# Decode part of a hybrid mLSTM and sparse-attention step: loads and stores in another order, and two compressions inside the state loop

## The chip, the cores and the metric

The kernel runs on one core of a Trainium2 chip. The core has five engines that run their own instruction streams and meet at semaphores: TensorE (PE in the rows; PEld is its weight load), VectorE (DVE), ScalarE (ACT), GpSimd (POOL) and SyncE (SP). SP does no arithmetic; it issues the transfers between HBM and the on-chip memory. ACT can issue transfers too, on a queue of its own. A row whose engine is SPq or ACTq is such an issue. The metric is the time of one execution on the device in microseconds; lower is better.

## The reference, cut to what matters

One layer, for two groups of requests that share the weights: a prompt of 1024 tokens, and a decode group of 8 requests ("samples") with 4 new tokens each, 32 rows in all, over a cache of 1024 tokens per sample. The part that the change touches is the decode group:

```python
# mLSTM heads: a matrix state per sample b and head h, 128 x 128
num = einsum('bthd,..', w, vc) + inter * einsum('bhvk,bthk->bthv', C, qc)   # needs C transposed
C   = decay * C + einsum('bsh,bshv,bshk->bhvk', wk, vc, kc)                 # the state update

# sparse attention heads: three branches over the cache
past_cmp = cache_kv_cmp[layer, page_table]                    # 8 pages of 128 tokens per sample
first, second = cmp_sub(past_cmp, w_cmp)                      # compression: einsum('bnpchd,cpde->bnche')
kv_c = compress_blocks(...)                                   # then scores on kv_c, top-16 blocks,
o = g0 * o_compressed + g1 * o_selected(cache_kv_sel) + g2 * o_window(cache_kv_win)

y = concat(h_m * silu(z_m), o_n * silu(z_n)) @ w_out          # merge, for prompt and decode rows
out = x + rmsnorm(y, g_post)
```

`w_out` is 1024 x 1024 in float32, 4 MB. The merge of the prompt's 1024 rows needs it whole.

## The kernel before, in words

The program is written by hand, one instruction stream for each engine (`@block.sync`, `@block.gpsimd`, `@block.scalar`, `@block.vector`, `@block.tensor`); nothing reorders it. Every stream runs in the order of its text, and a `wait_ge` holds up all that stands behind it on that engine. The prompt is projected and its attention done first. The decode part begins near 860 us of the profiled span, and runs in four stages.

1. **Set-up, 864 to 905 us.** SP loads the decode rows, the four heads of the matrix state (`c_in[h]`, 512 KB each, to `c_all[h]`), and the pages of `cache_kv_cmp` of sample b (`load_cmp(b)`, L700 to L706: 8 transfers of 128 KB, each with the page number read from the page table into a register first, L697). They go to one of four slots, `cms`: three in the big buffer WR, the fourth in a piece of XT called `pairs3`. POOL sorts a loaded sample (`sort_sample`), and counts it in `cm_sorted`. (The count has one more than the samples sorted, since the prompt's own block is counted too.)
2. **Compression.** For pair q (sample q-1) PE turns the sorted block (`turn_sample`, L2051, 16 transposes; in two halves of 8 by the program's own order), ACT copies it out of PSUM (`take_sample`, L1115), PE multiplies by the compression weights (`sample_products`, L2068, two groups of 8 matmuls, counted in `cmp_done`), DVE adds the shifted halves (`sum_sample`, L1529 and L1531), PE turns the values (`turn_values`, L2078) and DVE copies them (`take_values`, L1539). q = 1 to 5 stand in the set-up; q = 6 to 8 and the last products stand behind the state loop.
3. **State loop, 905 to 931 us.** For each of 4 heads: PE transposes the state of the 8 samples into banks 2 and 3 (L2275), ACT copies that to `ct_h` (L1236), DVE spreads the keys (`kblk`, L1707) and multiplies the old state by its decay (`c_dec`, L1714), PE forms the update in four matmuls that use 32 rows each and write banks 0, 1, 4 and 5 (L2284), DVE adds it (L1720, counted in `cn_ready`), and PE makes the numerator (L2287, L2290: 8 matmuls 4 columns wide, counted in `num_done`). SP stores the new state (L781).
4. **Attention over the selected and window pages, and the merge, 959 us to the end.** Two groups of four samples. PE's stream is a list of attention steps ("gates", "cmp", "u0" to "u11", ...), and `fill(n)` puts n matmuls of the merge (L2326, 512 columns wide) between them; 128 such in all. `fill` waits for `wo_in` at its first matmul (chunks 0 to 5 of `w_out` in WR) and for `wo_late` at its seventh (chunks 6 and 7, whose place holds the compression weights until the last compression). Step "u0" waits until 32 pages of `cache_kv_sel` have landed (`page_in`; four buffers, one over the state of heads 0 and 1, one over heads 2 and 3, two free earlier). DVE's first piece of the merge (`scale_rows`, L1748 and L1750) waits for the last small loads of SP (`gp_in`).

What sets the order of the transfers is SP's text. Behind the state loop it reads: chunks 0 to 3 of `w_out` (L730), stores of the state (L781), the last page loads (L713), which wait until all four heads are stored, then chunks 4 and 5 and chunks 6 and 7 (L734), windows (L725), `g_post` (L800), rows of `x` (L803) and eight small loads (L806, L807).

## Time and profile before

| | us |
|---|---|
| median of 3 runs | 1140.92 |
| lowest and highest | 1140.73, 1146.22 |
| the profiled execution, its own time | 1149.3 |
| its span, first to last instruction | 1147.5 |
| PE busy in it | 1063.9 (93%) |
| DVE, ACT, POOL busy | 474.1, 337.0, 68.5 |
| mean granted clock of TensorE | 0.957 |

The profile gives busy time by engine, groups of instructions by line, and, on asking, every instruction in order of time with the idle time before it and what ended that. "Granted clock" is the share of TensorE's full 2.4 GHz that the chip let through; 0.50 is 1.2 GHz. All terms below are sums within the profiled execution, whose own time is 8.4 us above the median of the runs.

### The profile page before, as it was taken

How to read it: one execution, taken by the hardware profiler on the slowest of the kernel's cores; microseconds unless marked ns; L12 is line 12 of the kernel's file. 1: busy time of each engine (PE TensorE's matmuls, PEld its weight loads, DVE VectorE, ACT ScalarE, POOL GpSimd, SP SyncE). 2: the span in 40 equal slices, each digit the busy share in tenths (PEclk: the TensorE clock that was granted, in tenths of full speed). 3: DMA queues.
4: the chain of work that ended last, by engine and by line, in shares of the span. 5: the costliest groups of instructions: out<-in, count | busy, mean ns of one | idle time of the engine just before them, and what ended most of it. 6: DMA issues, size and time to landing. Idle time of an engine off the chain costs nothing.

```text
span 1147.5 us, 14594 instructions
## 1 busy us (share of the span) xinstructions
PE 1063.9 (93%) x5369; PEld 640.9 (56%) x5369; DVE 474.1 (41%) x1045; ACT 337.0 (29%) x816; POOL 68.5 (6%) x173
## 2 busy tenths in 40 slices
PE   5999999999999999999978999999998893599997
PEld 4556654444445555786654456666567793245443
DVE  6444440000121221223247777677664532244442
ACT  5321110000011111111036676767665220022121
POOL 1000000000000000120011000001005100000000
PEclk9999999999999999999979999999998767799999
DMA  9302020203020151521031000000005344722512
GB/s 331 139 2 74 1 73 1 66 28 76 1 76 19 29 117 33 121 58 51 1 97 51 2 1 2 1 1 2 1 1 155 105 142 147 220 87 93 189 37 79
DMA packets 84205, 77.62 MB, mean 68 GB/s; under 512 B 29394, under 2 KB 68734, under 8 KB 84070
## 3 DMA queue, kind: packets, MB, share of 16 engines
q1 hardware_dynamic: 73654, 65.12, 18.9%
q10 hardware_dynamic: 10480, 11.57, 3.9%
q8 instruction: 43, 0.70, 0.2%
q14 instruction: 28, 0.23, 0.1%
HBM read 66.72 MB, written 14.10 MB: 70 GB/s over the span
## 4 chain that ended last, share of the span: by engine, by line
PE 77%; SPq 9%; DVE 6%; issue 3%; ACT 2%; DMA 2%; ACTq 0%; POOL 0%; DVEq 0%; POOLq 0%
PE PS L2021 26%; PE PS L2014 13%; PE PS L2326 8%; PE PS L2135 6%; PE PS L2154 5%; PE PS L2167 5%; SPq L697 2%; SPq L706 2%; SPq L713 1%; DMA out_s_C<-KVN 1%; PE PS L2355 1%; PE PS L2141 1%; PE PS L2186 1%; DVE XT L1582 1%; DMA KTR<-in_x_sample 1%
## 5 line engine op out<-in xcount | busy, mean ns | idle before, releaser
L2021 PE MATMUL PS<-WR,XT 128*128 128x512 f32 (+1 forms) x768 | 306.9, 557 | 0.0
L2021 PEld LDWEIGHTS PS<-WR,XT 128*128 128x128 f32 x768 | 144.0, 190 | 147.7 <-issue 144.6
L2014 PE MATMUL PS<-XT,WR 128*128 128x352 f32 x576 | 173.9, 463 | 2.1 <-ACT QN L1028 2.1
L2014 PEld LDWEIGHTS PS<-XT,WR 128*128 128x128 f32 x576 | 109.7, 192 | 63.0 <-ACT QN L1028 2.6
L1571 DVE TENSOR_REDUCE XT<-PS 128x1 f32<-128x640 f32 (+7 forms) x128 | 84.4, 701 | 30.2 <-PE PS L2141 29.7
L2326 PE MATMUL PS<-WR,QT 128*128 128x512 f32 x128 | 63.9, 621 | 24.5 <-DMA WR<-in_w_out 24.5
L2135 PE MATMUL PS<-KTR,XT 64*128 64x512 f32 (+3 forms) x384 | 84.8, 502 | 0.4 <-ACT XT L1149 0.2
L1149 ACT ACTIVATE XT<-PS,XT 128x640 f32<-128x640 f32 (+7 forms) x96 | 66.7, 701 | 10.6 <-DVE XT L1571 10.6
L2154 PE MATMUL PS<-cst,XT 128*128 128x128 f32 x396 | 62.1, 281 | 4.4 <-DVE XT L1582 3.6
L2326 PE MATMUL PS<-WR,KT 128*128 128x512 f32 x128 | 61.0, 598 | 0.0
L2135 PEld LDWEIGHTS PS<-KTR,XT 64*128 64x128 f32 x384 | 40.1, 192 | 28.4 <-issue 17.9
L1582 DVE TENSOR_SCALAR XT<-XT,small 128x640 f32<-128x640 f32 (+7 forms) x96 | 53.5, 557 | 3.5
L1162 ACT ACTIVATE MT<-PS 128x512 f32<-128x512 f32 (+3 forms) x96 | 41.1, 466 | 45.3 <-PE PS L2154 45.1
L2154 PEld LDWEIGHTS PS<-cst,XT 128*128 128x128 f32 x396 | 42.6, 142 | 17.8 <-issue 10.0
L1162 ACT ACTIVATE VV<-PS 128x512 f32<-128x512 f32 (+3 forms) x96 | 41.3, 469 | 32.0 <-PE PS L2154 31.9
L2326 PEld LDWEIGHTS PS<-WR,QT 128*128 128x128 f32 x128 | 23.2, 196 | 47.5 <-DMA WR<-in_w_out 24.6
L1407 DVE SCALAR_TENSOR_TENSOR KTR<-KTR,PS 128x512 f32<-128x512 f32 x8 | 5.5, 687 | 104.1 <-ACT KTR L1051 104.1
L2326 PEld LDWEIGHTS PS<-WR,KT 128*128 128x128 f32 x128 | 22.9, 192 | 23.5 <-issue 23.3
L2167 PE MATMUL PS<-MT,KVN 128*64 128x256 f32 x264 | 34.9, 390 | 0.8 <-ACT MT L1162 0.8
L1028 ACT ACTIVATE QN<-PS 128x352 f32<-128x352 f32 (+1 forms) x24 | 10.7, 457 | 84.1 <-PE PS L2014 83.2
L2167 PE MATMUL PS<-VV,KVN 128*64 128x256 f32 x264 | 35.1, 391 | 0.0
L1254 ACT ACTIVATE KTR<-PS 128x512 f32<-128x512 f32 x16 | 9.5, 594 | 85.7 <-PE PS L2326 85.6
(457 smaller groups left out, 1246.5 us busy)
## 6 DMA issues: line engine op xcount, KB each, us to landing
WR<-in_w_in SPq DMA_DIRECT2D x24, 512.0 KB, 7.9
WR<-in_cache_kv_cmp SPq DMA_DIRECT2D x48, 128.0 KB, 2.5
MT<-row_factors ACTq DMA_DIRECT2D x16, 256.0 KB, 7.3
WR<-in_w_in SPq DMA_DIRECT2D x32, 128.0 KB, 3.3
QN<-in_cache_kv_win SPq DMA_DIRECT2D x8, 512.0 KB, 7.6
out_y_prompt<-MT ACTq DMA_DIRECT2D x8, 512.0 KB, 2.9
out_s_kv_win<-in_cache_kv_win SPq DMA_DIRECT2D x1, 4064.0 KB
XT<-in_x_prompt ACTq DMA_DIRECT2D x6, 512.0 KB, 4.2
```

The lines of the kernel that those rows point to most:

```text
L697: return sp.value_load(table[0:1, b * NPG + n:b * NPG + n + 1], min_val=0, max_val=I["cache_kv_cmp"].shape[1] - 1)
L706: sp.dma_start(cms[b % 4][n % 2 * 64:n % 2 * 64 + 64, n // 2, :], src).then_inc(cm_s_in[b % 4], 16)
L1149: nc.scalar.activation(pp[p % 2][h][:, 0:nb * P], bank(score_bank(p, h), -(-nb // 4))[:, 0:nb * P], ACT.Exp, bias=nmax[:, u % 4:u % 4 + 1] ...
L1162: nc.scalar.activation(pt[q % 2][:, h, j:j + n, g % 2 * P:(g % 2 + 1) * P], bank(4 + y % 2)[:, 0:n * P].rearrange("p (k t) -> p k t", k=n) ...
L1571: nc.vector.tensor_reduce(nmax[:, u % 4:u % 4 + 1], bank(score_bank(p, h), -(-nb // 4))[:, 0:nb * P], AX.X, ALU.max, negate=True).then_inc ...
L1582: nc.vector.tensor_scalar(pp[p % 2][h][:, 0:nb * P], pp[p % 2][h][:, 0:nb * P], s1, gates[:, i, gc:gc + 1], op0=ALU.mult, op1=ALU.mult).th ...
L2014: ins = mm(b[:, 0:THIRD], w[:, k, r // 3 * P:(r // 3 + 1) * P], xt[:, k, r % 3 * THIRD:(r % 3 + 1) * THIRD], **f)
L2021: ins = mm(b[:, 0:width], xt[:, k, r * P:(r + 1) * P], w[:, k, :], **f)
L2135: mm(bank(score_bank(p, h) + j // 4)[:, 0:n * P], qz[r, i % 2, g, :], ktr[r, br, (k0 + j) * P:(k0 + j + n) * P], start=True, stop=not (j + ...
L2154: ins = nc.tensor.transpose(bank(4 + y % 2)[:, k * P:(k + 1) * P], pp[p % 2][h][:, (j + k) * P:(j + k + 1) * P], ident)
L2167: ins = mm(bank(6)[h * ND:(h + 1) * ND, x], v, pt[q % 2][:, h, k, :], start=False, stop=br == 1 and k == nb - 1, skip_group_check=True)
L2326: ins = mm(bank(2 + 3 * half), (qt if c < 4 else kt)[:, c % 4, i * P:(i + 1) * P], wo[:, c, half * 512:half * 512 + 512], start=c == 0, st ...
```

## The change

Five things, all in the decode part.

- **w_out by ACT.** Chunks 0 to 5 are issued by ACT, behind its work for the state loop, when all samples are sorted (`cm_sorted` 9). Chunks 6 and 7 stay with SP, and stand behind the windows.
- **SP's order.** Each head's state is stored among the page loads, pages over heads 0 and 1 wait only for the stores of these two, and so for 2 and 3; the page numbers of the first group are read into registers early (`held`, while SP has nothing else), and those of the second group at the place where SP waits for the first. Sample 7 is loaded to slot 0, not to slot 3, and before the page loads.
- **Buffers.** `pairs3` now holds two copies of the transposed state (`cts`), one for even and one for odd heads. `c_dec` and `kblk` move to STG.
- **The update** is two matmuls of 512 columns, in banks 2 and 3 that the transposes used, where it was four of 256 in four other banks. So PE's transposes of the next head wait for DVE's addition (`cn_ready`), and the update's matmuls wait for ACT's copies (`ct_ready`). The decode values are loaded to 2 groups of 32 partitions, where it was 4.
- **Compressions in the loop.** Banks 0, 1, 4 and 5 are free in the loop, and one half of `turn_sample` and one half of `sample_products` stand in each head: pairs 6 and 7 turned, pairs 5 and 6 multiplied.

```diff
+        cts = [pairs3[:, n * 1024:(n + 1) * 1024].rearrange("p (b k) -> p b k", b=SB) for n in range(2)]
+        slot = lambda b: b % 4 if b < 7 else 0
...
+            def store_state(h):
+                sp.wait_ge(cn_ready, h + 1)
+                sp.dma_start(O["s_C"][:, :, h, :, :].rearrange("l b v k -> v (l b) k"), c_all[h]).then_inc(c_in[h], 16)
...
-            held = [[page(4 + j, n) for n in range(NPG)] for j in range(4)]
+            held = [[page(j, n) for n in range(NPG)] for j in range(4)]
...
             load_cmp(7)
+            load_pages((3,))
+            store_state(0)
+            store_state(1)
             sp.wait_ge(f_pe, 3)
             load_pages((1,))
-            sp.wait_ge(cm_sorted, 7)
-            for c in range(4):
-                load_wo(c)
-            for h in range(MH):
-                sp.wait_ge(cn_ready, h + 1)
-                sp.dma_start(O["s_C"]...).then_inc(c_out, 16)
+            store_state(2)
+            store_state(3)
...
+            for h in range(2):
+                sp.wait_ge(c_in[h], 2 * 16)
+            load_pages((0,))
+            for h in range(2, MH):
+                sp.wait_ge(c_in[h], 2 * 16)
+            load_pages((2,))
+            sp.wait_ge(s_outs, 20 * 16)
+            sp.dma_start(gpost, ...)
             sp.wait_ge(num_done, MH)
-            sp.wait_ge(c_out, MH * 16)
-            load_pages((0, 2))
-            sp.wait_ge(cm_sorted, 8)
-            load_wo(4)
-            load_wo(5)
+            for i in range(2):
+                sp.dma_start(xr[:, i, :], ...)
+            sp.wait_ge(cmp_done, 2 * SB)
+            load_windows(0)
             sp.wait_ge(cmp_done, 2 * (SB + 1))
             load_wo(6)
             load_wo(7)
-            load_windows(0)
...
+            held = [[page(4 + j, n) for n in range(NPG)] for j in range(4)]
             sp.wait_ge(kb_turned, 8)
             load_half(0, page_in)
@@ scalar @@
             for h in range(MH):
                 for half in range(2):
                     act.wait_ge(c_turned, 2 * h + half + 1)
-                    if h and half == 0:
-                        act.wait_ge(num_done, h)
+                    if h >= 2 and half == 0:
+                        act.wait_ge(num_done, h - 1)
...
+                take_sample(6 + h // 2, (2 * (h % 2), 2 * (h % 2) + 1))
+            act.wait_ge(cm_sorted, 9)
+            for c in range(6):
+                load_wo(c)
+            take_sample(8)
@@ vector @@
+                tt(c_all[h], c_dec, bank(2, 2)..., ALU.add).then_inc(cn_ready, 1)
+                if h + 1 < MH:
+                    spread_keys(h + 1)
+                if h == 2:
+                    take_values(5, vc_all[4])
+                sum_sample(5 + h // 2, (h % 2,))
@@ tensor @@
                 if h:
-                    pe.wait_ge(ct_ready, 2 * h)
+                    pe.wait_ge(cn_ready, h)
...
+                turn_sample(6 + h // 2, (2 * (h % 2), 2 * (h % 2) + 1))
+                if h == 2:
+                    turn_values(5)
+                sample_products(5 + h // 2, (h % 2,))
                 pe.wait_ge(kblk_ready, h + 1)
+                pe.wait_ge(ct_ready, 2 * h + 2)
                 v = us_all[:, 3, h * P:(h + 1) * P]
-                for r in range(4):
+                for r in range(2):
                     rr = slice(r * NS, (r + 1) * NS)
+                    ins = mm(bank(2 + r), v[rr, :], kblk[rr, :, :], start=True, stop=True)
```

On PE, the state loop's first head and the start of the second, before (L2275 the state's transposes, L2284 the update, L2287 and L2290 the numerator):

```order
L2275 MATMUL PS<-cst,GM 128x128 x8
L2284 MATMUL PS<-KTR,MT 128x256 x4
L2287 MATMUL PS<-XT,MT 128x32
L2290 MATMUL PS<-XT,VV 128x4 x8
L2275 MATMUL PS<-cst,GM 128x128 x8
```

and the same place now (L2286 the transposes, L2064 a half of `turn_sample`, L2081 a half of `sample_products`, L2298 the update):

```order
L2286 MATMUL PS<-cst,GM 128x128 x8
L2064 MATMUL PS<-cst,VV 128x128 x8
L2081 MATMUL PS<-QN,WR 128x128 x8
L2298 MATMUL PS<-STG,MT 128x512 x2
L2301 MATMUL PS<-XT,MT 128x32
L2303 MATMUL PS<-XT 128x4 x8
L2286 MATMUL PS<-cst,GM 128x128 x8
```

Sixteen instructions of the compression now stand in each head, and the update is two wide matmuls.

On SP, from the state's stores to the small loads, before; the two gaps hold page loads and the issues that repeat:

```order
L730 DMA WR<-in_w_out 128x1024 x4
L781 DMA out_s_C<-GM 128x8x128 x2
L781 DMA out_s_C<-KVN 128x8x128 x2
L783 DMA out_s_m<-XT 4x8x1
...
L734 DMA WR<-in_w_out 64x1024 x8
L725 DMA QN<-in_cache_kv_win 128x4x256 x4
L800 DMA MT<-in_g_post 128x1024
L803 DMA XT<-in_x_prompt 128x1024 x2
L806 DMA KTR<-in_g_post 32x256
```

and now:

```order
L735 DMA out_s_C<-GM 128x8x128 x2
...
L735 DMA out_s_C<-KVN 128x8x128 x2
L782 DMA out_s_m<-XT 4x8x1
...
L792 DMA MT<-in_g_post 128x1024
L795 DMA XT<-in_x_prompt 128x1024 x2
L725 DMA QN<-in_cache_kv_win 128x4x256 x4
L730 DMA WR<-in_w_out 64x1024 x4
L804 DMA KTR<-in_g_post 32x256
```

Eight of the twelve issues for `w_out` have left SP's queue, and the four that stay have moved from ahead of the windows to behind them.

On ACT, behind the last copies of the state loop, now (the line of `w_out` stood nowhere on ACT before; L1114 is `take_sample`):

```order
L1243 ACTIVATE XT<-PS 128x512 x2
L1114 ACTIVATE QN<-PS 128x512 x2
L1232 DMA WR<-in_w_out 128x1024 x4
L1236 DMA WR<-in_w_out 64x1024 x4
L1114 ACTIVATE VV<-PS 128x512 x4
```

The eight issues stand between the last copy of pair 7 and the copies of pair 8.

## Rows read from the trace of the kernel before

**Rows 1.** Timeline of PE, state loop: start, length, instruction, [idle before <-releaser].

```profile
905.11 1.43 PE L2275 MATMUL PS<-cst,GM 128*128 128x128 f32 x8 [0.59 <-DVE XT L1539]
...
911.32 1.95 PE L2275 MATMUL PS<-cst,GM 128*128 128x128 f32 x8
913.20 1.24 PE L2284 MATMUL PS<-KTR,MT 32*128 32x256 f32 x8
...
914.61 3.57 PE L2290 MATMUL PS<-XT,VV 128*128 128x4 f32 x16
918.05 1.95 PE L2275 MATMUL PS<-cst,KVN 128*128 128x128 f32 x8
```

**Rows 2.** Timeline of PE, from the loop's end to the merge.

```profile
931.57 0.79 PE L2294 MATMUL PS<-XT,MT 32*128 32x128 f32 x2
...
945.94 1.04 PE L2051 MATMUL PS<-cst,VV 128*128 128x128 f32 x8
...
947.54 1.96 PE L2068 MATMUL PS<-QN,WR 128*128 128x128 f32 x16
949.34 1.04 PE L2051 MATMUL PS<-cst,VV 128*128 128x128 f32 x8
950.21 1.95 PE L2068 MATMUL PS<-QN,WR 128*128 128x128 f32 x16
...
958.86 0.40 PE L2369 MATMUL PS<-XT 32*128 32x24 f32 x2
983.73 3.78 PE L2326 MATMUL PS<-WR,QT 128*128 128x512 f32 x4 [24.47 <-DMA WR<-in_w_out]
...
1001.77 1.12 PE L2355 MATMUL PS<-cst,KVN 128*128 128x128 f32 x4 [4.27 <-DVE VV L1785]
```

**Rows 3.** Timeline of SP: its issues, merged by line.

```profile
920.94 9.11 SPq L706 DMA_DIRECT2D XT<-in_cache_kv_cmp  x8
...
944.26 5.57 SPq L781 DMA_DIRECT2D out_s_C<-KVN  x2
...
959.10 8.12 SPq L713 DMA_DIRECT2D GM<-in_cache_kv_sel  x8
...
976.42 4.99 SPq L734 DMA_DIRECT2D WR<-in_w_out  x8
981.45 3.05 SPq L725 DMA_DIRECT2D QN<-in_cache_kv_win  x4
...
1016.51 8.10 SPq L720 DMA_DIRECT2D GM<-in_cache_kv_sel  x16
```

**Rows 4.** The chain that ended last: start, length, what.

```profile
948.37 9.79 DMA out_s_C<-KVN
...
992.55 7.79 DMA KTR<-in_x_sample
...
1008.88 1.72 PE PS L2326 x4
```

**Rows 5.** Stretches: PE, PEld, DVE, ACT, POOL busy, granted clock, DMA share, GB/s.

```profile
902.00:904.00 2.00, 0.20 (x1) 0.00 (x0) 1.55 (x5) 0.00 (x0) 0.00 (x0) 1.00 0.25 79
...
906.00:908.00 2.00, 2.00 (x14) 1.44 (x12) 0.59 (x2) 1.02 (x2) 1.69 (x4) 0.50 0.37 110
...
936.00:938.00 2.00, 2.00 (x19) 2.00 (x18) 0.79 (x4) 0.13 (x1) 0.00 (x0) 0.91 0.26 88
...
948.00:950.00 2.00, 2.00 (x21) 2.00 (x20) 0.39 (x3) 0.03 (x1) 0.00 (x0) 1.00 1.15 347
```

**Rows 6.** The same view, later and over a longer stretch.

```profile
960.00:980.00 20.00, 0.00 (x0) 0.00 (x0) 0.00 (x0) 0.00 (x0) 0.00 (x0) 0.51 0.46 132
...
984.00:986.00 2.00, 2.00 (x3) 0.90 (x4) 0.00 (x0) 0.00 (x0) 0.00 (x0) 0.50 1.03 227
```

**Rows 7.** Timeline of DVE, first head of the loop.

```profile
907.85 1.28 DVE L1720 TENSOR_TENSOR GM<-VV,PS 128x512 f32<-128x512 f32 x2 [1.41 <-PE PS L2284]
```

**Rows 8.** DMA issues: KB each, median us from issue to landing.

```profile
WR<-in_w_out SPq DMA_DIRECT2D x8, 256.0 KB, 5.7
```

More of the change, by code:

```diff
@@ L89 @@
 S_PAIR = S_SAME + P
-S_END = S_PAIR + 2
+S_END = S_PAIR + 4
 def constant_tables():
@@ L332, in build @@
         gr = from_x(NS + SB)
-        ga_s = from_x(4 * NS)
+        ga_s = from_x(2 * NS)
         grb = from_x(MH * (NS + SB))
@@ L711, in load_pages @@
                     for n in range(NPG):
-                        src = I["cache_kv_sel"][0, bass.ds(page(j, n), 1), :, :, :, :]
+                        src = I["cache_kv_sel"][0, bass.ds(held[j][n], 1), :, :, :, :]
                         sp.dma_start(pages[j][:, n, :], src.rearrange("o p x h d -> (o p) (x h d)")).then_inc(page_in, 16)
@@ L796, in _ @@
             load_wo(7)
-            load_windows(0)
-            sp.wait_ge(s_outs, 20 * 16)
-            sp.dma_start(gpost, I["g_post"].partition_broadcast(P)).then_inc(gp_in, 16)
-            sp.wait_ge(cm_sorted, SB + 1)
-            for i in range(2):
-                sp.dma_start(xr[:, i, :], xf[i * P:(i + 1) * P, :]).then_inc(xr_in[i], 16)
             for j in range(4):
@@ L1229, in _, with load_wo @@
             take_sample(5, (2, 3))
-            act.wait_ge(cmp_done, 2 * 5)
+            def load_wo(c):
+                if c < 4:
+                    act.dma_start(wo[:, c, :], I["w_out"][0, c * P:(c + 1) * P, :]).then_inc(wo_in, 16)
+                else:
+                    for h in range(KVH):
+                        r = DM + (h * GQ + c - 4) * ND
+                        act.dma_start(wo[h * ND:(h + 1) * ND, c, :], I["w_out"][0, r:r + ND, :]).then_inc(wo_in, 16)
             for h in range(MH):
@@ L1732, in _ @@
             tt(am_s, hx(dens), gts, ALU.mult).then_inc(f_dve, 1)
-            for q in range(5, SB + 1):
+            take_values(6, vc_all[5])
+            for q in range(7, SB + 1):
                 sum_sample(q)
```

108 lines of the change are left out of this document (42 added, 66 removed).

## The prediction, on record before the changed kernel ran

> **What bounds the kernel now.** I read the busy times first: PE is busy 93% of the span, so a gain must come out of PE's idle time, or out of time in which PE runs at half its clock. The stretches and PE's timeline behind 860 us show where both lie. There are two long waits: 24.47 us ahead of the merge's first matmul, ended by the landing of `w_out` (PE stood still from 959.3 to 983.7), and 4.27 us at 1001.77, the fourth key step "u3" [rows 2]. The chain says what was behind the second: a small load that landed 7.79 us after its issue, and held up DVE's first piece of the merge [rows 4]. The first has a longer story in SP's timeline. SP issued the last stores of the state till 949.8, waited until the last had landed (9.79 us after 948.37 [rows 4]), issued sixteen page loads from 959.1 to 976.4, and only then the rest of `w_out` [rows 3]. So PE waits for SP's order, not for the amount of data: from 960 to 980 the DMA engines were busy for 0.46 of the time and moved 132 GB/s [rows 6]. The third thing is the clock. PE stood nearly still at 902 to 904, and from 906 to 936 the clock was at 0.50, 1.2 GHz; it came back as the first turns and products of a compression ran behind the loop; [rows 5] has the first and the last of these stretches. The whole state loop ran at half speed: a head took 6.73 us (911.32 to 918.05) [rows 1]. Behind u3 PE is busy almost without a gap, so whatever moves u3 moves the end.
>
> So the sum is made for one point: when does u3 start. Before, 1001.77.
>
> **PE's own path to u3.** Prices at full clock, from start to start in [rows 2]: half a turn 0.87 (949.34 to 950.21), half of the products 1.80 (947.54 to 949.34). From the loop at half clock [rows 1]: transposes 1.88 (so 0.94 at full clock, and 0.87 by the same eight transposes of a turn; I take 0.87), update with the small matmul behind it 1.41 (913.20 to 914.61), numerator 3.44 (914.61 to 918.05), half of which is 1.72. The new update streams 2 x 512 columns. The trace has only the four of 256, of which 1.41 us of half clock is an upper end if nothing changes, 0.70 at full clock; if the four ran beside each other and the two do too, each is twice as long, 1.4 at full clock. I take 1.2, nearer the second.
>
> - A head at full clock: 0.87 + 0.87 + 1.80 + 1.2 + 1.72 = 6.46.
> - The first head starts at 905.1, since what releases it is the same, with its clock falling as before. Transposes 1.4, half a turn at half clock 1.9, products between 1.8 and 3.6, say 2.7 (the clock is back after about three such microseconds behind the loop in [rows 5]), 1.2, 1.7: 8.9, to 914.0.
> - Three more heads, 19.4: 933.4. The sums for the denominator (L2294 and its neighbour, 931.57 to 932.9 at half clock) 0.7: 934.1.
> - The rest, pair 8 turned, pair 7 and 8 multiplied, stands unchanged from 945.94 to 958.86 [rows 2]: 12.9, with its waits for DVE. Gates at 947.0, against 958.86.
>
> DVE doesn't come to bound the loop: addition 1.28 [rows 7], decay of the same 1024 elements about as long, keys of the next head under 1, half a `sum_sample` about 1: some 4.5 of 6.46 us. The new wait of PE's transposes for the addition is covered by the numerator: the addition ends 1.28 and a little behind the update, the numerator takes 1.72. Without that cover (a numerator at nothing) it would cost 1.3 in each of three heads.
>
> From gates to u3 stand eleven merge matmuls, 0.86 each (1.72 for two [rows 4]), and three key steps and the scores, some 2.3: 11.8. So PE alone would have u3 at 958.8.
>
> **Transfers to u3.** The chain is now: last addition, store of head 3, its landing, last eight page loads, `g_post`, two `x` loads, windows, chunks 6 and 7, small loads.
>
> - SP's earlier work: sample 7 was issued from 920.94 and took 9.11 [rows 3]; eight page loads stood ahead of it, and they are behind it now. So sample 7 goes from about 911 to 920, pages 3 to 924. A page load whose number is held costs 0.51 (8.10 for 16) against 1.02 (8.12 for 8) [rows 3], so eight cost 4.1. Stores 0 and 1, pages 1: about 930. Sorted by 925, sample 7 is in time for its turn at 934.
> - The fourth addition ends 1.9 us ahead of the numerator's end, plus 1.3 and some 0.2: 933.0. The store lands between 5 and 9.8 us later [rows 4], I take 8, since ACT's weights run beside it: 941. Pages 945. `g_post`, `x` 1.5; windows 3.05 [rows 3]; four chunk issues at 0.62, 2.5: 952. All their waits on PE (products of pair 7, of pair 8 at 945) are met by then. The landing takes 5.7 [rows 8]: 958 by latency.
> - By volume it is later. From 930, when ACT has issued its copies and begins, there are to move: chunks 0 to 5, 3 MB; the last stores, 0.8; pages 0 and 2, 2; `g_post` 0.5; `x` 1; windows 2; chunks 6 and 7, 1: 10.3 MB. The DMA engines, all busy, moved 347 GB/s of page and store traffic, but 227 GB/s of the half-height chunks [rows 5, 6]. 8.3 MB at 347 is 24, 2 MB at 227 is 9: 33 us, to 963. I take 962 for chunks 6 and 7; the ends are 957 and 968.
>
> So PE comes to the seventh merge matmul at 947.0 + 1.7 + 0.5 + 3.4 + 0.5 = 953.1, and waits about 9 us there, with the clock down for the first 3 us behind, as behind both waits before. From there: 1.8 + 1.0 + 2.7 + 0.44 + 1.7 = 7.7, with a little for the small loads: u3 at 970. That is 31.8 earlier than 1001.77. What ran at half clock behind u3 before (some 3 us, gone now) is 1.7 more. **Sum: 33**, so 1149.3 becomes 1116, and the median of the runs 1140.9 becomes 1108.
>
> What could be late next: SP reads 32 page numbers behind the small loads, 32 x 0.51 (1.02 less 0.51) = 16 us, to about 976. The step it then serves stood 14.7 us behind u3 (1016.51 [rows 3]), now 985. Nothing is lost, and these pages are needed 50 us later. `w_out` by ACT: eight issues, about 4 us, in front of the copies of pair 8; the turn they follow comes at 934. At nothing as long as the queue takes them; if it blocks as SP's stores did (5.57 for two [rows 3]) some 3 to 5 us.
>
> A rule speaks against the update's new form. The Trainium skill (TensorE: Matmul & The Clock Gate, Why this matters for your kernels) says that matmuls of 32 rows in distinct row groups run concurrently. By it two groups in place of four double the update's time; this would put the head 0.2 above my figure, under 1 us in all. No row of before shows the two-group form.
>
> **Rivals.**
>
> - *Transfers hidden.* The DMA engines keep up, and u3 comes when PE gets there, 959 to 965. Saving 38 to 45: 1096 to 1103. For it: the DMA share in the loop was 0.25 to 0.37 [rows 5]. Against: the volume above.
> - *The clock falls again in each head.* The numerator at its 4 columns went with a clock of 0.50 throughout the old loop [rows 1, 5]. If it falls there and returns in the products, a head is 3 to 3.5 us longer, the last addition 10 later, and the chain of transfers with it, less the 2 or 3 of volume it had to wait for anyway. Saving 22 to 28: 1113 to 1119.
> - *Half clock for the whole loop.* A head takes 1.88 + 1.88 + 3.6 + 2.6 + 3.44 = 13.4, the last addition is at 955, u3 at 983. Saving 18 to 21: 1120 to 1123.
> - *ACT's load is in the way.* The 3 MB of weights and the store of head 3 share the DMA engines, and the store comes last: its landing takes 8 + 9 (3 MB at 347 GB/s [rows 5]) = 17 us, all behind it is up to 9 later, u3 at 979. Saving 24: 1117. For it: stores took 9.8 us beside 2 MB of weights [rows 4]. Against: SP's transfers were then behind the weights in one queue. The Trainium skill (DMA: Bandwidth & Descriptors, Issuing engines are not separate DMA queues) has transfers issued by SP and by ACT on the same 16 engines, interleaved, so that a second issuer saves issue time alone. By that, this rival would be as likely as the forecast; the trace has no stretch with both.
> - *Slower.* The clock stays down past the loop, through the tail and into the merge. Loop to 957.6 with the denominator; tail's 10.3 busy microseconds doubled, 981; eleven merge matmuls at 1.9 and the key steps doubled, u3 at 1005; and another ten microseconds at half clock behind it, 5: 1149. It decides if the clock has not come back by the key steps. Against it: turns and products brought it back within 4 us behind the old loop [rows 5].
>
> **How the numbers follow.** Forecast, 1103 to 1113: 0.50. Hidden 0.13. Clock falls in each head, or ACT's load is in the way: 0.23. Half clock in the whole loop 0.09. Within 0.5% (5.7 us, about what a measurement of this kernel can tell from no change) 0.03, slower 0.02. The range 1098 to 1120 leaves out half of "hidden", most of half clock, and the last two: under 0.2.
>
> **What would show it.** Right: no wait of PE at the merge's first matmul above 3 us, one of 5 to 12 us at the seventh, ended by `w_out` issued by SP; a head of 6 to 7 us with the clock at 1.00 from the second on; the last store of the state issued near 933; u3 near 970. Wrong: a head of 10 to 13 us; a wait of PE's transposes for DVE in the loop; SP still reading page numbers when the eighth key step is done; a first merge wait over 5 us.

## The result, and the profile after

| | before | changed |
|---|---|---|
| median of 4 runs, us | 1143.35 | 1128.35 |
| lowest and highest | 1140.73, 1146.22 | 1126.1, 1128.7 |
| ratio, 95% interval | | 0.985, 0.982 to 0.988 |
| profiled execution, own time and span | 1149.3, 1147.5 | 1126.1, 1124.3 |
| TensorE's mean granted clock | 0.957 | 0.980 |

The change makes the kernel faster by 15.0 us. The forecast was 33, and 1128 lies outside the range of 1098 to 1120. The page of the changed kernel, busy time by engine, still has PE at 93%:

```profile
PE 1045.0 (93%) x5353; PEld 623.7 (55%) x5353; DVE 474.3 (42%) x1041; ACT 335.9 (30%) x816; POOL 69.5 (6%) x173
```

PE's timeline of the changed kernel, state loop (start, length, instruction, and in brackets the idle time before it and what ended that), to be read beside [rows 1]:

```profile
899.41 1.04 PE L2286 MATMUL PS<-cst,GM 128*128 128x128 f32 x8
900.29 1.04 PE L2064 MATMUL PS<-cst,VV 128*128 128x128 f32 x8
901.16 1.95 PE L2081 MATMUL PS<-QN,WR 128*128 128x128 f32 x16
903.04 1.13 PE L2298 MATMUL PS<-STG,MT 32*128 32x512 f32 x4
904.00 0.30 PE L2301 MATMUL PS<-XT,MT 32*128 32x32 f32 x2
904.23 1.95 PE L2303 MATMUL PS<-XT 128*128 128x4 f32 x16
906.04 1.07 PE L2286 MATMUL PS<-cst,GM 128*128 128x128 f32 x8
...
930.68 1.06 PE L2064 MATMUL PS<-cst,VV 128*128 128x128 f32 x8 [0.81 <-ACT VV L1114]
```

The first head takes 6.63 us (899.41 to 906.04) with half a compression's turn and half of another's products inside it, and no bracket stands in it: PE waits for nothing. The same timeline from the gates to u3, to be read beside [rows 2]:

```profile
940.23 0.40 PE L2376 MATMUL PS<-XT 32*128 32x24 f32 x2
940.84 1.98 PE L2333 MATMUL PS<-WR,QT 128*128 128x512 f32 x4 [0.21 <-DMA WR<-in_w_out]
...
955.21 1.11 PE L2362 MATMUL PS<-cst,GM 128*128 128x128 f32 x4 [8.40 <-DMA KVN<-in_cache_kv_sel]
972.03 2.08 PE L2333 MATMUL PS<-WR,KT 128*128 128x512 f32 x2 [15.71 <-DMA WR<-in_w_out]
...
979.68 0.60 PE L2362 MATMUL PS<-cst,KVN 128*128 128x128 f32 x4
```

The 24.47 us at the merge's first matmul have shrunk to 0.21, and the 4.27 at u3 are gone. In their place stand 8.40 us at u0, for the pages in the buffer over heads 2 and 3, and 15.71 at the merge's seventh matmul, for chunks 6 and 7. SP's timeline tells why these came late; it answers to [rows 3]:

```profile
917.92 4.09 SPq L713 DMA_DIRECT2D KVN<-in_cache_kv_sel  x8
922.05 1.19 SPq L735 DMA_DIRECT2D out_s_C<-GM  x2
923.42 7.16 SPq L713 DMA_DIRECT2D GM<-in_cache_kv_sel  x8
930.63 7.41 SPq L735 DMA_DIRECT2D out_s_C<-KVN  x2
938.08 2.65 SPq L782 DMA_DIRECT2D out_s_m<-XT  x1
...
941.47 5.79 SPq L713 DMA_DIRECT2D GM<-in_cache_kv_sel  x8
949.03 3.95 SPq L713 DMA_DIRECT2D KVN<-in_cache_kv_sel  x8
...
954.44 4.56 SPq L725 DMA_DIRECT2D QN<-in_cache_kv_win  x4
959.04 4.05 SPq L730 DMA_DIRECT2D WR<-in_w_out  x4
```

The same eight page loads with numbers already held cost 4.09 us at 917.92 and 7.16 at 923.42, and two stores cost 1.19 and then 7.41. ACT's eight issues began at 923.22 (4.09 and 2.49 us for four each). In the view of DMA issues from 920 to 975 (KB each, median us from issue to landing), the last stores took 17.3 us to land:

```profile
WR<-in_w_out ACTq DMA_DIRECT2D x4, 256.0 KB, 10.3
out_s_C<-KVN SPq DMA_DIRECT2D x2, 512.0 KB, 17.3
WR<-in_w_out SPq DMA_DIRECT2D x4, 256.0 KB, 8.8
```

And the stretches (the last three columns are granted clock, DMA share, GB/s): the loop at full clock, ACT's chunks of 128 rows, the half-height chunks 6 and 7, and the whole stretch from ACT's first issue to the landing of chunks 6 and 7.

```profile
926.00:928.00 2.00, 2.00 (x17) 1.86 (x17) 1.47 (x6) 0.00 (x0) 0.00 (x0) 1.00 0.96 293
...
930.00:932.00 2.00, 1.32 (x12) 1.34 (x13) 1.55 (x7) 1.68 (x4) 0.00 (x0) 1.00 1.04 412
...
966.00:968.00 2.00, 0.00 (x0) 0.00 (x0) 0.00 (x0) 0.00 (x0) 0.00 (x0) 0.50 1.02 209
...
922.00:972.00 50.00, 22.36 (x146) 16.71 (x144) 12.22 (x40) 2.87 (x7) 1.19 (x2) 0.77 0.98 276
```

For 50 us the DMA engines were busy for 0.98 of the time; before, they had been busy for 0.46 in PE's long wait [rows 6]. PE's long wait was set by SP's order before; now it is set by the transfers themselves and by what stands in front of what.

**One measure for all runs.** The decode part begins with SP's first load of the decode rows, at 864.48 us in the first trace of before and at 861.06 in the changed kernel's. That difference has nothing to do with the change (a second trace of before, below, has 860.27, a second one of the changed kernel 863.87), so times are given here from that point. The forecast u3 of 970, in the first trace's time, is 105.5 us behind it; measured was 118.6. From u3 to the end of the span it is 144.6 us (979.68 to 1124.3), and before 145.7: what moves u3 moves the end, as the prediction had it. The traces of all runs ("gates" is the step ahead of the merge, "u3" the fourth key step):

| kernel | gates | merge's 7th matmul | u3 | u3 to end | median, us |
|---|---|---|---|---|---|
| before, first trace | 94.4 | 127.3 | 137.3 | 145.7 | 1143.35 |
| before_again | 86.3 | 126.4 | 135.9 | 146.0 | 1144.93 |
| changed | 79.2 | 111.0 | 118.6 | 144.6 | 1128.35 |
| after_again | 80.7 | 112.7 | 119.6 | 144.7 | 1128.57 |
| w_thin | 81.0 | 102.5 | 111.1 | 144.6 | 1118.84 |
| windows_last | 78.9 | 104.2 | 112.0 | 144.6 | 1122.26 |
| loop_alone | 98.5 | 111.4 | 118.6 | 144.7 | 1126.89 |
| before_act | 96.2 | 110.9 | 124.1 | 146.6 | 1135.12 |
| w_full_height | 79.9 | 135.8 | 142.9 | 144.6 | 1152.83 |
| w_early | 82.6 | 103.6 | 111.6 | 144.6 | 1120.61 |
| best | 79.7 | 124.0 | 130.6 | 144.7 | 1141.82 |
| w_by_sp | 82.5 | 112.7 | 119.9 | 144.6 | 1129.04 |
| best2 | 78.3 | 92.2 | 100.7 | 144.7 | 1108.97 |
| best2_loop_alone | 99.2 | 105.8 | 111.3 | 144.6 | 1120.18 |

The kernels were measured in four groups, each beside runs of before. before_again was one execution, 1143.96, and its line has the median of before in its group. Before had 1143.35 beside the changed kernel; 1144.93 beside before_again, loop_alone, w_thin and windows_last; 1145.11 beside before_act, w_full_height, w_early and best; 1147.16 beside the other four. The ratios below are to these. Before's medians differ by up to 3.8 us from group to group, the changed kernel's two by 0.2; u3, behind the decode start, moved by 1.0 and 1.4 between two traces of one kernel.

### The profile page after: what moved, and what is told of

Same layout as the page of the kernel before. It is cut to its first block, busy times and chain, and to the rows that moved or that the text cites. A ratio compares the mean times of both kernels' runs of the same rounds, so it can differ in the third digit from the quotient of the medians.

```text
span 1124.3 us, 14552 instructions
## 1 busy us (share of the span) xinstructions
PE 1045.0 (93%) x5353; PEld 623.7 (55%) x5353; DVE 474.3 (42%) x1041; ACT 335.9 (30%) x816; POOL 69.5 (6%) x173
## 3 DMA queue, kind: packets, MB, share of 16 engines
q1 hardware_dynamic: 72470, 61.84, 18.6%
## 4 chain that ended last, share of the span: by engine, by line
PE 79%; SPq 7%; DVE 6%; DMA 3%; issue 3%; ACT 2%; ACTq 0%; POOL 0%; DVEq 0%; POOLq 0%
PE PS L2034 27%; PE PS L2027 14%; PE PS L2333 9%; PE PS L2148 6%; PE PS L2167 5%; PE PS L2180 5%; SPq L706 2%; DMA out_s_C<-KVN 2%; SPq L697 1%; SPq L713 1%; DMA WR<-in_w_out 1%; PE PS L2154 1%; PE PS L2362 1%; PE PS L2032 1%; DVE XT L1591 1%
## 5 line engine op out<-in xcount | busy, mean ns | idle before, releaser
L2034 PEld LDWEIGHTS PS<-WR,XT 128*128 128x128 f32 x768 | 144.0, 190 | 147.7 <-issue 144.6
L1580 DVE TENSOR_REDUCE XT<-PS 128x1 f32<-128x640 f32 (+7 forms) x128 | 84.4, 701 | 30.3 <-PE PS L2154 29.8
L2333 PE MATMUL PS<-WR,QT 128*128 128x512 f32 x128 | 61.2, 599 | 0.2 <-DMA WR<-in_w_out 0.2
L2167 PEld LDWEIGHTS PS<-cst,XT 128*128 128x128 f32 x396 | 42.6, 141 | 18.0 <-issue 10.8
L1798 DVE COPY VV<-PS 128x512 f32<-128x512 f32 x24 | 16.5, 689 | 46.4 <-PE PS L2362 46.3
L2333 PEld LDWEIGHTS PS<-WR,QT 128*128 128x128 f32 x128 | 22.6, 191 | 23.2 <-issue 22.8
```

What stands on the lines that cost most here:

```text
L1580: nc.vector.tensor_reduce(nmax[:, u % 4:u % 4 + 1], bank(score_bank(p, h), -(-nb // 4))[:, 0:nb * P], AX.X, ALU.max, negate=True).then_inc ...
L1798: nc.vector.tensor_copy(ktb[:, kk % 4, :], bank(4)).then_inc(ktb_ready, 1)
L2034: ins = mm(b[:, 0:width], xt[:, k, r * P:(r + 1) * P], w[:, k, :], **f)
L2167: ins = nc.tensor.transpose(bank(4 + y % 2)[:, k * P:(k + 1) * P], pp[p % 2][h][:, (j + k) * P:(j + k + 1) * P], ident)
L2333: ins = mm(bank(2 + 3 * half), (qt if c < 4 else kt)[:, c % 4, i * P:(i + 1) * P], wo[:, c, half * 512:half * 512 + 512], start=c == 0, st ...
```

## The experiments

After the result my theory was that of the fourth rival: ACT's 3 MB get in front of the last stores and all that waits for them. Against it stood the order of SP's own transfers, the loop's pace, and a first trace of before that was not typical.

**before_again.** The kernel before, unchanged, traced once more.

> The kernel before, once more, for its profile. Theory N (the traced execution of before was an unlucky one): the 8 us between its 1149.3 and the fastest run 1140.7 sit in a stretch that the change leaves alone or in its waits for transfers, and a second trace gives about 1141 to 1146 with the decode part's start (first SP issue of the decode rows, 864.5 in the first trace) near 861. Theory T (tracing costs a fixed 6 to 8 us): the second trace gives 1149 again with the same start.

It took 1143.96 us, its decode part began at 860.27, and its loop ran faster than in the first trace:

```profile
946.55 0.40 PE L2369 MATMUL PS<-XT 32*128 32x24 f32 x2
978.40 3.78 PE L2326 MATMUL PS<-WR,QT 128*128 128x512 f32 x4 [31.45 <-DMA WR<-in_w_out]
...
996.13 0.95 PE L2355 MATMUL PS<-cst,KVN 128*128 128x128 f32 x4 [3.75 <-DVE VV L1785]
```

The gates came 8.1 us earlier, behind the decode start, than in the first trace, the wait behind them was 7.0 us longer, and u3 came 1.4 us earlier. The granted clock in the loop was not the same either: 0.67 on average from 904 to 930, where the first trace had 0.50. So PE's pace in the loop was hidden behind SP's order in before, and the changed kernel gains 17.2 us at u3 by this trace and 18.7 by the first. The medians give 15.0, and 18.6 for after_again, beside which before had 1147.16.

**w_thin.** ACT's eight loads keep their place and number, and each brings 8 of 1024 columns.

```diff
-                    act.dma_start(wo[:, c, :], I["w_out"][0, c * P:(c + 1) * P, :]).then_inc(wo_in, 16)
+                    act.dma_start(wo[:, c, 0:8], I["w_out"][0, c * P:(c + 1) * P, 0:8]).then_inc(wo_in, 16)
...
-                        act.dma_start(wo[h * ND:(h + 1) * ND, c, :], I["w_out"][0, r:r + ND, :]).then_inc(wo_in, 16)
+                        act.dma_start(wo[h * ND:(h + 1) * ND, c, 0:8], I["w_out"][0, r:r + ND, 0:8]).then_inc(wo_in, 16)
```

> The changed kernel, but ACT loads only 8 of the 1024 columns of the w_out chunks 0 to 5 (part of the weights is left out), at the same place and with the same semaphores. Theory A (ACT's 3 MB crowd SP's queue: page loads 1 took 7.2 instead of 4.1, two stores 7.4, the small store 2.7, so that the last pages came at 953): without them SP's stores and loads issue unblocked, the last store is issued near 927, pages 2 end near 937, chunks 6 and 7 land near 955, the wait at the seventh merge matmul falls from 15.7 to under 6 us and the wait for pages from 8.4 to under 2: 1109 to 1114. Theory B (SP's own small descriptors of the stores block it, whoever else loads): the issues keep their lengths, and the time stays at 1124 to 1129.

Measured 1118.84 us (ratio to before 0.977, 0.975 to 0.979), 9.5 below the changed kernel. One line of its DMA view, and PE's timeline:

```profile
out_s_C<-KVN SPq DMA_DIRECT2D x2, 512.0 KB, 5.8
```

```profile
949.96 0.60 PE L2362 MATMUL PS<-cst,GM 128*128 128x128 f32 x4
965.34 2.07 PE L2333 MATMUL PS<-WR,KT 128*128 128x512 f32 x2 [14.77 <-DMA WR<-in_w_out]
```

The last stores land in 5.8 us in place of 17.3, and the wait at u0 is gone. Chunks 6 and 7 come 8.5 us earlier. But 14.77 us of the wait for them stay, since PE now comes to them without the wait at u0: ACT's data are 8.5 us of the 13.5 by which these chunks missed their forecast, and not all of it. The expected 1109 to 1114, with a wait under 6 us, was not reached. SP's issue of pages 1 still took 6.01 us (5.58 in w_by_sp below, where no weights were under way yet), so ACT's data are only a part of what slowed that; the two stores behind it took 1.58 in place of 7.41.

**windows_last.** The four window loads, 2 MB, move from ahead of chunks 6 and 7 to behind the small loads.

```diff
-            sp.wait_ge(cmp_done, 2 * SB)
-            load_windows(0)
             sp.wait_ge(cmp_done, 2 * (SB + 1))
...
                 sp.dma_start(xr_s[r, :], xs[:, c]).then_inc(gp_in, 16)
+            load_windows(0)
```

> The changed kernel with the four window loads of the first group (2 MB) moved from ahead of w_out's chunks 6 and 7 to behind the eight small loads; nothing else. Theory V (volume in SP's queue ahead of chunks 6 and 7 sets the wait): 2 MB at 227 to 347 GB/s are 6 to 9 us, the wait at the seventh merge matmul falls from 15.7 to 7 to 10, u3 comes 6 to 9 earlier: 1119 to 1122. Theory L (the landing of the chunks is limited by something else, such as their half-height form): no change, 1127 to 1129.

Measured 1122.26 (0.981, 0.979 to 0.984), 6.1 below the changed kernel; chunks 6 and 7 come 6.8 us earlier, and the waits are 1.08, 6.14 at u0 and 9.03 at the seventh matmul. The windows in front of chunks 6 and 7 are a second cause of PE's wait, as large as 2 MB at a common rate (2 MB in 6.8 us is 308 GB/s). These bytes are no cause of the miss, since the forecast's sum had them in front too.

**loop_alone.** The changed kernel, but the compression work of pairs 5 to 7 stands behind the state loop, as before; everything else (ACT's loads, SP's order, buffers, the two-group update) as in the changed kernel. The core of the diff against it, on PE:

```diff
-                turn_sample(6 + h // 2, (2 * (h % 2), 2 * (h % 2) + 1))
-                if h == 2:
-                    turn_values(5)
-                sample_products(5 + h // 2, (h % 2,))
```

> The changed kernel with the compressions of pairs 5 to 7 back behind the state loop on all engines; transfers and buffers as changed. If the products in the loop keep the clock up: the loop runs at 0.50 again, a head takes 6.7 to 7.5 us, and the gates step comes 10 to 14 later than 940. Because sample 7 can then only be sorted behind the loop, ACT's weights come some 15 us later too, and the wait for them is back: 1133 to 1142. Rival (the compressions' place is worth nothing, since PE waits for transfers anyway): within 3 us of the changed kernel.

Measured 1126.89 (0.984, 0.981 to 0.986), no different from the changed kernel, where I had expected 1133 to 1142. The loop ran at half clock, with a wait for ACT's copy in each head; PE's timeline:

```profile
910.35 2.08 PE L2291 MATMUL PS<-STG,MT 32*128 32x512 f32 x4 [0.78 <-ACT XT L1243]
912.18 0.47 PE L2294 MATMUL PS<-XT,MT 32*128 32x32 f32 x2
912.59 3.58 PE L2296 MATMUL PS<-XT 128*128 128x4 f32 x16
...
962.40 2.44 PE L2331 MATMUL PS<-WR,QT 128*128 128x512 f32 x4 [1.68 <-DMA WR<-in_w_out]
...
973.24 1.33 PE L2331 MATMUL PS<-WR,KT 128*128 128x512 f32 x2 [2.84 <-DMA WR<-in_w_out]
```

The gates come 19.3 us later than in the changed kernel and u3 at the same 118.6, since the waits behind them are 4.5 us in place of 24.3. With the transfers as they stand in the change, the compressions in the loop bring nothing in sum. But the two kernels come to the same u3 by different ways, for the edit moves transfers too. ACT's timeline, then SP's:

```profile
945.10 0.39 ACTq L1232 DMA_DIRECT2D WR<-in_w_out  x1
```

```profile
943.74 0.90 SPq L795 DMA_DIRECT2D XT<-in_x_prompt  x2
953.65 5.10 SPq L725 DMA_DIRECT2D QN<-in_cache_kv_win  x4
```

ACT's weights start at 945.10, not at 923.22, so the last stores landed in 5.4 us and SP had its page loads out by 943.22, behind the decode start 10.6 us earlier than in the changed kernel. It then stood 9.0 us before the windows (943.74 and 0.90, then 953.65), for the products of pair 7. What the stores gained, SP's wait for PE took back. That the two come out equal is a coincidence of this order, and this run does not price the loop by itself.

**before_act.** The kernel before, with chunks 0 to 5 issued by ACT behind its copies for the loop's first head, and no other edit.

```diff
-            sp.wait_ge(cm_sorted, 7)
-            for c in range(4):
-                load_wo(c)
...
-            load_wo(4)
-            load_wo(5)
...
+                if h == 0:
+                    act.wait_ge(cm_sorted, 8)
+                    for c in range(4):
+                        act.dma_start(wo[:, c, :], I["w_out"][0, c * P:(c + 1) * P, :]).then_inc(wo_in, 16)
```

> The kernel before, with one part of the change alone: chunks 0 to 5 of w_out issued by ACT, behind its first head's copies in the state loop, when cm_sorted is 8. SP's order is as before without them. Theory S (the order and page numbers on SP set what is late): the merge's first matmul no longer waits (24 to 31 us before), but PE then waits for the pages, whose issues end near 976 as before, and for chunks 6 and 7: the key step u0 waits about 20 us, and u3 comes 4 to 8 us earlier than before: 1136 to 1141. Theory W (late weights alone were the stall): 1115 to 1125.

Measured 1135.12 (0.991, 0.988 to 0.994): 10.0 us faster than before, a little more than I expected. The wait at u0, expected at about 20 us, was 2.95: the last stores landed in 6.7 us (9.5 in the first trace of before), and SP's last page loads were issued by 966.5, not near 976. The wait at the first matmul is gone; others take its place, and ACT's place costs the loop 3.76 us once:

```profile
914.15 3.58 PE L2291 MATMUL PS<-XT,VV 128*128 128x4 f32 x16 [3.76 <-ACT VV L1229]
...
968.17 1.11 PE L2356 MATMUL PS<-cst,GM 128*128 128x128 f32 x4 [2.95 <-DMA KVN<-in_cache_kv_sel]
...
973.66 2.07 PE L2327 MATMUL PS<-WR,KT 128*128 128x512 f32 x2 [4.37 <-DMA WR<-in_w_out]
...
986.81 1.11 PE L2356 MATMUL PS<-cst,KVN 128*128 128x128 f32 x4 [5.38 <-DVE VV L1786]
```

This edit alone gives two thirds of the 15.0 us of the whole change.

**w_early.** Of the changed kernel, chunks 2 to 5 are issued by ACT behind its copies of the loop's second head, when sample 6 is sorted, and chunks 0 and 1 stay at the end.

```diff
+                if h == 1:
+                    act.wait_ge(cm_sorted, 8)
+                    for c in range(2, 6):
+                        load_wo(c)
             act.wait_ge(cm_sorted, 9)
-            for c in range(6):
+            for c in range(2):
                 load_wo(c)
```

> The changed kernel with chunks 2 to 5 of w_out issued by ACT behind its second head's copies (cm_sorted 8, near 909, where the DMA share was 0.1 to 0.2); chunks 0 and 1 stay behind the loop. Theory A (ACT's weights crowd the last stores and the pages behind them): the last stores land within 9 us in place of 17, pages 2 are issued by 946 in place of 953, chunks 6 and 7 land 6 to 9 us earlier: 1119 to 1123. Rival (total volume until chunks 6 and 7 is fixed and begins to flow at 920 either way): under 3 us of gain.

Measured 1120.61 (0.978, 0.975 to 0.981), 7.7 below the changed kernel. The last stores landed in 7.4 us, the wait at u0 is gone, 14.35 us stay at the seventh matmul. It is nearly the picture of w_thin, with all weights loaded: two of the three megabytes moved to a time when the DMA engines had little to do (a share of 0.21 from 908 to 910 in the changed kernel). In this trace the clock fell in three heads of the loop, on the same PE instructions that ran at 1.00 in the changed kernel:

```profile
905.74 1.95 PE L2290 MATMUL PS<-cst,GM 128*128 128x128 f32 x8
...
915.41 1.95 PE L2290 MATMUL PS<-cst,KVN 128*128 128x128 f32 x8
```

This head took 9.67 us, and the gates came 3.4 us later than in the changed kernel; the wait for chunks 6 and 7 hid that.

**w_full_height.** Chunks 4 to 7 are loaded as one transfer of 128 partitions each, where they are two of 64.

```diff
-                for h in range(KVH):
-                    r = DM + (h * GQ + c - 4) * ND
-                    sp.dma_start(wo[h * ND:(h + 1) * ND, c, :], I["w_out"][0, r:r + ND, :]).then_inc(wo_late, 16)
+                src = I["w_out"][0, DM:DM + DM, :].rearrange("(h g r) n -> g h r n", h=KVH, g=GQ)[c - 4, :, :, :]
+                sp.dma_start(wo[:, c, :], src).then_inc(wo_late, 16)
```

> The changed kernel with each of the chunks 4 to 7 of w_out loaded by one transfer of 128 rows in place of two of 64; same bytes, same places. If the half-height form is what held the traffic to 209 to 237 GB/s at 1.02 to 1.07 share while they ran: those stretches come to 340 or more, 2 MB take 6 us in place of 9, and the seventh merge matmul's weights land 2 to 4 us earlier: 1124 to 1127. If it is the traffic around them: unchanged, 1127 to 1129.

Measured 1152.83 (1.006, 1.004 to 1.008): slower than before, where I expected a gain. PE waited 17.58 us at the first and 29.80 at the seventh matmul. A stretch of 2 us in which DMA moved next to nothing but such a chunk (the next 2 us read the same):

```profile
948.00:950.00 2.00, 0.00 (x0) 0.00 (x0) 0.00 (x0) 0.00 (x0) 0.00 (x0) 0.50 0.13 53
```

53 GB/s at a share of 0.13, which is about two of sixteen engines. The source and the destination are written with an outer dimension of 2. The Trainium skill (DMA: Bandwidth & Descriptors, Why a DMA increments its semaphore by 16 and not by 1) says that a transfer is spread over the largest number of engines up to 16 that divides the slowest dimension of both its sides. By that, it is two engines here, and the trace agrees. Of these two forms, two transfers of 64 rows are the better one. ACT's two slow chunks were under way when SP issued the stores of heads 2 and 3, which landed in 26.6 us. The question of the run, whether 64 rows in a transfer are what holds its rate down, stays open.

**best.** w_early, w_full_height, chunks 6 and 7 ahead of the last pages, and the windows last.

> All together: w_early, w_full_height, and on SP chunks 6 and 7 right behind the pages over heads 0 and 1, then pages over heads 2 and 3, g_post, the small loads, x rows, windows last. If the volume ahead of each need was the limit, the two waits (pages 8.4, chunks 15.7) fall to under 3 us each and PE's own path shows: gates near 940, u3 near 956 to 960: 1107 to 1113. If waits only change their names (pages 2 now behind chunks 6 and 7): 1115 to 1120.

Measured 1141.82 (0.997, 0.995 to 0.999). It has the same fault as w_full_height: PE waited 30.61 us for the pages behind the two-engine chunks. It says nothing on the order it was meant for; best2 does.

**after_again and w_by_sp.** The changed kernel once more, and the changed kernel with ACT's eight issues moved to SP, ahead of the stores of heads 2 and 3.

```diff
             load_pages((1,))
+            sp.wait_ge(cm_sorted, 9)
+            for c in range(6):
...
+                    sp.dma_start(wo[:, c, :], I["w_out"][0, c * P:(c + 1) * P, :]).then_inc(wo_in, 16)
...
             store_state(2)
             store_state(3)
...
-            act.wait_ge(cm_sorted, 9)
-            for c in range(6):
-                load_wo(c)
```

> The changed kernel once more, as the base of this comparison: 1126 to 1130, with PE's waits of 8 us for pages and 15 us for chunks 6 and 7 ahead of the merge's seventh matmul.

> The changed kernel, but SP issues chunks 0 to 5, between page loads 1 and the store of head 2, in place of ACT. Theory R (both issuers feed the same DMA engines, so that only the issue time moves): the weights stand ahead of the last stores in one queue; stores of heads 2 and 3 land 9 to 10 us after issue as in the kernel before, pages 2 end near 955, and the time is within 4 us of the changed kernel, 1126 to 1132. Theory I (issue by ACT is what helps): 1133 or more.

Measured 1128.57 and 1129.04 (0.983 and 0.984 of before). The waits are 9.10 and 15.43, and 7.03 and 15.73; the last stores landed in 15.9 and 14.4 us. Who issues the weights is worth 0.5 us, within the scatter. (I had expected 9 to 10 us for the landing in w_by_sp, as in before; it was 14.4 with the weights in front in the same queue.) The Trainium skill (DMA: Bandwidth & Descriptors, Issuing engines are not separate DMA queues) has the transfers of all issuers on the same 16 DMA engines, interleaved, so that a second issuer saves issue time alone; this pair agrees.

**best2.** w_early with the halves of the chunks as they were, and chunks 6 and 7 right behind the last pages, then `g_post`, the small loads, the rows of `x`, and the windows last.

```diff
             load_pages((2,))
-
-            sp.wait_ge(s_outs, 20 * 16)
-            sp.dma_start(gpost, I["g_post"].partition_broadcast(P)).then_inc(gp_in, 16)
...
-            sp.wait_ge(cmp_done, 2 * SB)
-            load_windows(0)
             sp.wait_ge(cmp_done, 2 * (SB + 1))
...
             load_wo(7)
+
+            sp.wait_ge(s_outs, 20 * 16)
+            sp.dma_start(gpost, I["g_post"].partition_broadcast(P)).then_inc(gp_in, 16)
...
+            sp.wait_ge(num_done, MH)
+            for i in range(2):
+                sp.dma_start(xr[:, i, :], xf[i * P:(i + 1) * P, :]).then_inc(xr_in[i], 16)
+            load_windows(0)
```

> w_early, and on SP chunks 6 and 7 right behind the pages over heads 2 and 3, then g_post, small loads, x rows, windows last; chunks 4 to 7 as two transfers of 64 rows each, as in the changed kernel. If each effect adds (w_early 8 us, windows 6): 1113 to 1116, wait at the seventh merge matmul 5 to 8. If PE's own path is reached sooner: no lower than 1107. If w_early and windows_last remove the same wait: 1119 to 1122.

Measured 1108.97 (1107.45 to 1109.98; 0.967 of before, 0.963 to 0.971), below the 1113 to 1116 expected if the two effects only add. It beats both kernels, the changed one by 19.6 us. PE's timeline, then two lines of its stretches:

```profile
938.63 0.40 PE L2379 MATMUL PS<-XT 32*128 32x24 f32 x2
...
948.08 0.85 PE L2365 MATMUL PS<-cst,GM 128*128 128x128 f32 x4 [3.15 <-DMA KVN<-in_cache_kv_sel]
952.50 2.07 PE L2336 MATMUL PS<-WR,KT 128*128 128x512 f32 x2 [3.56 <-DMA WR<-in_w_out]
...
961.02 0.60 PE L2365 MATMUL PS<-cst,KVN 128*128 128x128 f32 x4
```

```profile
906.00:908.00 2.00, 2.00 (x20) 2.00 (x19) 1.63 (x3) 1.96 (x4) 0.00 (x0) 1.00 0.09 23
...
922.00:972.00 50.00, 40.45 (x201) 24.89 (x200) 19.23 (x60) 5.62 (x12) 2.28 (x4) 0.90 0.85 242
```

The waits of 24.1 us have become 6.7. Four of ACT's chunks now start at 907 to 911, where the DMA engines stood at 0.09, and PE works for 40.45 of the 50 us from 922 on, where it worked for 22.36.

**best2_loop_alone.** best2 with the compressions behind the loop, as in loop_alone.

> best2 with the compressions of pairs 5 to 7 back behind the state loop. If PE waits for transfers in best2 no longer than about 7 us, the loop's place now counts: the merge starts 15 to 20 us later (960), u3 some 8 to 13 us later than in best2: 1122 to 1128. If transfers still set the pace: within 3 us of best2.

Measured 1120.18 (0.976, 0.972 to 0.980), 11.2 slower than best2. I had expected 1122 to 1128. PE has no wait between gates and u3 here, so its own path sets the time: its gates come 20.8 us later than in best2 and u3 10.6. So the compressions in the loop, worth nothing in the changed kernel, are worth 11 us once the transfers are out of the way. The clock is part of this price: the loop had 1.00 in best2's trace and 0.50 in this one.

## Why the prediction was right, and where it was wrong

**The bound, and the point u3: right.** The first wait was SP's order, and u3 set the end in every run: 144.6 to 144.7 us from u3 to the last instruction in all kernels that have the change's two-group update.

**PE's own path: right, and a little too dear.** Gates were forecast 82.5 us behind the decode start (947.0 less 864.5) and came at 79.2. The loop began 2.3 us earlier behind the decode start than in before's first trace, which the sum took over, and its first head, priced at 8.9 for a clock that would fall, took 6.63 at a clock of 1.00. The other heads were priced at 6.46 and took 6.66 to 6.77. That the clock held was in part luck: in after_again it fell in the first head, which took 7.82, and in w_early in three heads. The update with the small matmul behind it was taken at 1.2 and took 1.19 (903.04 to 904.23). At half clock the update alone took 1.83 in loop_alone (910.35 to 912.18), where the four narrow groups of before took 1.02 (here in before_again, at half clock too):

```profile
909.98 1.24 PE L2284 MATMUL PS<-KTR,MT 32*128 32x256 f32 x8
911.00 0.47 PE L2287 MATMUL PS<-XT,MT 32*128 32x32 f32 x2
```

That is 1.8 times as much. The Trainium skill (TensorE: Matmul & The Clock Gate, Why this matters for your kernels) says that matmuls of 32 rows in distinct row groups run concurrently, from which the prediction worked out twice; the traces nearly agree. The transposes never waited for DVE's addition. ACT's eight issues took 6.6 us, where about 4 were forecast, and cost PE 0.81, where the forecast was nothing, or 3 to 5 if the queue blocks.

**The waits of DVE on the small loads: right.** Nothing stands in front of u3 any more, and SP's 32 page numbers held nobody up.

**Transfers to u3: wrong, and this is the step that failed.** Chunks 6 and 7 were to be there 97.5 us behind the decode start (962), and PE got them at 111.0, 13.5 later. u3 is 13.1 late. By the prediction's own terms:

- *"The store lands between 5 and 9.8 us later ..., I take 8."* It landed in 17.3, at 949.0, 11.4 us behind the forecast's 941 (937.6 in this trace's time). This is the number of the rival "ACT's load is in the way" (8 + 9), whose rate was 9 us for 3 MB; w_thin, which takes the 3 MB away, gives back 8.5 us at the seventh matmul and 9.5 in the time. The prediction gave that rival and another one 0.23 together, for want of a stretch with both in it. The rival had the mechanism, but not all of the size: its u3 of 979 is 114.5 behind the decode start, 4.1 short of the measured 118.6, and its 1117 is 11 short. That the weights went by ACT's queue made no difference.
- *"so eight cost 4.1"* for pages 1, and the last stores at their issue, nothing beyond the wait for the addition. The addition was early (it ended at 925.6, 4.0 us ahead of the forecast's 929.6 in this trace's time), but SP was then in pages 1 for 7.16 us and in the stores for 7.41. The same kinds of issue cost 4.09 and 1.19 just before. The longer issues stand where the DMA share was near 1 (1.06 from 930 to 938); whether the queue or the DMA engines held them, no run separates. The stores fell back to 1.58 in w_thin; pages 1 stayed at 6.01 there and at 6.14 in best2.
- *"windows 3.05"* and *"four chunk issues at 0.62, 2.5"*. They took 4.56 and 4.05; without ACT's data still 4.92 and 3.81, in best2, where less stood in the queue, 2.52 and 2.43.
- *"10.3 MB"* in *"33 us"*. These are MB of 1024 KB, 10.8 million bytes, a mean of 327 GB/s. From 926.6 (930 in the first trace's time) to 971.6 there moved 280 GB/s for 45 us, 12.6 million bytes. So there were 1.8 million bytes more, since part of pages 1 and of the stores of heads 0 and 1 was still to move and the small loads were not counted, and the rate was lower. Each of the two is worth some 6 us, an estimate from these numbers. The 347 GB/s of [rows 5] was one slice of 2 us; by SP's issues and their landings only the last stores were in flight then, and 940 to 950 as a whole had 315. In w_thin, stores and page loads with hardly any weights beside them went at 232 GB/s at a share of 0.93 from 930 to 948.
- The wait of 8.40 us at u0 was not foreseen at all. It costs nothing of its own, as long as chunks 6 and 7 are later; it shows how late the pages were.

With a landing at 111.0, the rest follows as priced: from there to u3 it was 7.65 us, forecast 7.7 and a little.

**The other rivals.** The clock neither fell in each head nor stayed down in the changed kernel's two traces, so the two rivals on it and the slower case fell for this result. w_early's trace shows that such heads do occur (8.65, 9.67 and 8.32 us). "Transfers hidden" fell with the 15.71 us.

**The base.** The sum was made against a profiled execution of 1149.3, whose decode part began 3.4 us later than in the changed kernel's trace and 4.2 later than in its own second one. Counted from the decode start, the forecast gain at u3 was 31.8 us, 30.3 by the second trace, and the measured one 18.7 and 17.2. The term of 1.7 us behind u3 measured 1.1 (145.7 less 144.6). Between the two profiled executions the gain was 23.2 us (1149.3 to 1126.1), and 10 short of 33; between the medians it was 15.0, since the traced execution of before lay 6.0 above its median and the traced one of the changed kernel 2.3 below. So some 8 of the 18 us by which the saving fell short come from where the two traced executions lie against their medians, and 10 from the transfers (13.1 at u3, less the earlier decode start of 3.4).

**What the two halves of the change gave.** Without the compressions in the loop the kernel is as fast (loop_alone), so SP's order and ACT's issues are enough for the 15 us. The loop's part shows nothing in sum here, and 11.2 us in best2.

## What to carry to other kernels

When a wait of the bounding engine is moved from a queue's order to the transfers, add up the bytes that are then in flight, at the rate of their own form, and ask for each what stands in front of it, whatever queue it is on. Put what is needed late behind what is needed next, and start the rest where the DMA engines idle, even if its issuer is busy. A speed-up of the engine that waits shows only once its data are there: test the halves of a change with the other half mended, or a good one will be thrown away.

## What the runs showed of the hardware

- In the stretch in which chunks 6 and 7 landed, as transfers of 64 partitions (966 to 970 in the changed kernel), 209 to 237 GB/s moved at a share of 1.02 to 1.04; with rows of `x` and windows, on 128 partitions, 341 to 374 GB/s in best2 from 954 to 958 at 1.03 to 1.06. That the number of partitions makes the difference is not shown. A chunk as one transfer with an outer dimension of 2 moved 53.
- Two 512 KB stores of the state cost 1.19 us to issue at 922.05 and 7.41 at 930.63, where the DMA share was 1.06. Those of heads 2 and 3 landed 5.4 us after their issue (loop_alone) to 17.3 (changed kernel), and 26.6 in w_full_height.
- TensorE's clock stayed at 1.00 (2.4 GHz) through the state loop with turns and products in it in the changed kernel and in best2, but fell to 0.50 (1.2 GHz) in the first head of after_again and in three heads of w_early. Without turns and products it stood at 0.50 in loop_alone, and was 0.67 on average in before_again, whose first head ran at 1.00. PE was busy in all of them; why the clock fell in one and not in another, these runs don't settle.
